# A two-layer hybrid encoder: the second layer's output projection with tokens on partitions, its input turned in blocks, and one attention set moved

## The reference

```python
m = jax.nn.sigmoid(mg).reshape(B, S, N_BRANCH, D_MODEL)
y = m[:, :, 0] * za + m[:, :, 1] * zb + m[:, :, 2] * zc
x = x + y @ w_out            # per layer
...
return rmsnorm(x, final_g)   # behind the second layer
```

## Time and profile before

| | |
|---|---|
| median of 3 runs | 967.1 us (966.6 to 967.12) |
| profiled execution: its time | 966.41 us |
| its span, first to last instruction | 964.3 us |
| busy in it: TensorE matmuls, VectorE, ScalarE | 956.2, 572.5, 401.7 us |
| clock granted to TensorE, mean | 1.000 of full speed |

### The profile page before, as it was taken

The page is one execution under the profiler, slowest core; times in us unless marked ns, Lnnn a source line. Parts: engine busy times, 40 slices in busy tenths (PEclk is TensorE's granted clock), DMA queues, the critical chain, the costliest instruction groups (busy, mean ns, idle before and its releaser), DMA issues.

```text
span 964.3 us, 13421 instructions
## 1 busy us (share of the span) xinstructions
PE 956.2 (99%) x5438; PEld 789.0 (82%) x5438; DVE 572.5 (59%) x933; ACT 401.7 (42%) x747; POOL 0.9 (0%) x5
## 2 busy tenths in 40 slices
PE   9999999999999999999999999999999999999997
PEld 7988888888888877788888888888888887878887
DVE  7856465447656577375566654744565665754844
ACT  7443343225633356432435323431463424653324
POOL 0000000000000000000000000000000000000000
PEclk9999999999999999999999999999999999999999
DMA  7423323222234211122322432223213332112212
GB/s 282 139 73 128 110 68 122 95 92 84 66 106 125 87 67 45 67 88 89 103 92 88 128 121 93 86 89 107 71 64 109 109 121 66 48 64 69 99 51 88
DMA packets 30237, 91.60 MB, mean 95 GB/s; under 512 B 4384, under 2 KB 7200, under 8 KB 30048
## 3 DMA queue, kind: packets, MB, share of 16 engines
q1 hardware_dynamic: 29184, 89.74, 27.8%
q10 hardware_dynamic: 992, 1.00, 0.4%
HBM read 84.89 MB, written 2.23 MB: 90 GB/s over the span
## 4 chain that ended last, share of the span: by engine, by line
PE 95%; DVE 2%; ACT 1%; DMA 1%; SPq 1%; issue 0%; DVEq 0%
PE ring L612 73%; PE nat L612 8%; PE nat L850 3%; PE aux L891 2%; PE nat L857 1%; PE nat L829 1%; PE nat L864 1%; DMA raw<-pieces 1%; ACT work L1123 1%; PE aux L710 1%; DVE merged L1181 1%; PE ring L633 0%; PE ring L634 0%; PE ring L635 0%; PE nat L792 0%
## 5 line engine op out<-in xcount | busy, mean ns | idle before, releaser
L612 PE MATMUL ring<-act_hi,w_hi 128*128 128x512 f32 x832 | 328.9, 395 | 0.0
L908 ACT ACTIVATE w_hi<-raw 128x1024 fp32r<-128x1024 f32 x152 | 161.8, 1064 | 392.3 <-PE ring L612 357.6
L612 PE MATMUL ring<-act_lo,w_hi 128*128 128x512 f32 x832 | 324.2, 390 | 0.0
L612 PE MATMUL ring<-act_hi,w_lo 128*128 128x512 f32 x832 | 324.1, 390 | 0.0
L1203 DVE TENSOR_TENSOR w_lo<-raw,w_hi 128x1024 fp32r<-128x1024 f32 x152 | 185.2, 1219 | 50.9 <-ACT w_hi L908 50.7
L612 PEld LDWEIGHTS ring<-act_hi,w_hi 128*128 128x128 f32 x832 | 156.2, 188 | 36.1 <-issue 4.9
L612 PEld LDWEIGHTS ring<-act_hi,w_lo 128*128 128x128 f32 x832 | 156.2, 188 | 33.0
L612 PEld LDWEIGHTS ring<-act_lo,w_hi 128*128 128x128 f32 x832 | 156.3, 188 | 31.0
L1525 DVE SCALAR_TENSOR_TENSOR gates<-ring,rstd 128x512 f32<-128x512 f32 x72 | 49.7, 690 | 130.1 <-PE ring L612 130.1
L612 PE MATMUL ring<-y_hi,w_hi 128*128 128x512 f32 x192 | 74.7, 389 | 0.0
L612 PE MATMUL ring<-y_lo,w_hi 128*128 128x512 f32 x192 | 74.7, 389 | 0.0
(11 more groups left out here) (227 smaller groups left out, 990.2 us busy)
## 6 DMA issues: line engine op xcount, KB each, us to landing
raw<-pieces SPq DMA_DIRECT2D x152, 512.0 KB, 3.5
xt<-x_t SPq DMA_DIRECT2D x8, 256.0 KB, 4.8
bank_a<-work SPq DMA_DIRECT2D x32, 64.0 KB, 2.0
out_t<-gates SPq DMA_DIRECT2D x7, 256.0 KB, 2.3
rope<-tables SPq DMA_DIRECT2D x1, 1024.0 KB, 6.1
bank_a<-work SPq DMA_DIRECT2D x32, 32.0 KB, 2.0
raw<-pieces SPq DMA_DIRECT2D x2, 256.0 KB, 5.0
bank_g<-k_rope_dram SPq DMA_DIRECT2D x8, 64.0 KB, 3.2
```

Source lines behind the costliest of these rows:

```text
L612: mm = pe.matmul(dst, stationary, moving, start=start and i == 0, stop=stop and i == 2)
L908: nc.scalar.activation(w_hi[:, n % HL, :], raw[:, n % RAW, :], ACT.Copy).then_inc(hi_split.sem, 1)
```

## The change

The order: set 0 of branch C is issued behind nine quarters instead of ten, and two quarters follow its `turn_c`. The last `y_lo` comes four quarters earlier. Both hold for both layers.

In layer 1 a new entry `turn_x` lets VectorE transpose the residual stream in blocks of 32 x 32 (eight instructions of 128 x 512), into the free `bank_a`. Sixteen transfers of 128 KB on SP, in four batches ahead of four weight loads, put the blocks in place, so that `x_rows` holds the residual with tokens on the partitions, the features in the order `ROWS_ORDER`. The weights of this projection are packed in that order, and one transfer of 512 KB brings the gain, repeated on all partitions.

All eight pieces of the output projection of layer 1 then run in `last_rows`, with the activations stationary and the weights moving. The first four pieces give the first 512 features of all four groups of 128 tokens, in the four `nat` banks; the last four give the other 512 features, in the three ring banks and `aux`, and the last two pieces of these go group by group. The norm runs along the free axis: ScalarE squares with an accumulated sum, takes the root and scales the first half of the features, VectorE adds, multiplies by the gain, takes the reciprocal and scales the second half. Each group leaves in two transfers as soon as it is scaled, the last one's first half from ScalarE's queue. Pool has nothing to do. The host restores the order of the features.

```diff
-    quarters(10)
+    quarters(9)
...
-        quarters(1)
+        quarters(1 if y > 0 else 2)
     todo.append(("value_c", len(C_SETS) - 1))
     quarters(1)
     todo.append(("y_hi", 2 * TT - 1))
-    quarters(len(fill) - 1)
+    quarters(2)
     todo.append(("y_lo", 2 * TT - 1))
-    quarters(1)
+    todo.append(("turn_x", 0))
+    quarters(3)
+    todo.append(("turn_x", 1))
+    quarters(len(fill))
...
+        x_blocks = bank_a[:, 0:4096].rearrange("p (m t j c) -> p t m j c", m=4, t=TT, j=KT)
+        x_rows = bank_g[:, :].rearrange("p (t d) -> p t d", t=TT)
+        out_first = gates[:, 0:TT, :]
+        rows_raw, out_second = gates[:, TT:2 * TT, :], gates[:, 2 * TT:3 * TT, :]
+        gain = merged[:, 0:2, :]
+        squares = work[:, 0:TT, :]
+        row_ss, row_bias, row_rstd = sums[:, :, 0:2], recip[:, 0:TT], recip[:, TT:2 * TT]
...
+                if layer == DEPTH - 1 and PW <= p < PW + 4:
+
+                    m = p - PW
+                    sp.wait_ge(x_turned.sem, KT)
+                    for b in range(4):
+                        sp.dma_start(x_rows[32 * m:32 * m + 32, :, 256 * b:256 * b + 256],
+                                     bank_a[32 * b:32 * b + 32, 1024 * m:1024 * m + 1024].rearrange("p (t d) -> p t d", t=TT)
+                                     ).then_inc(rows_placed.sem, 16)
+                elif layer == DEPTH - 1 and p == PW + 4:
+                    sp.wait_ge(merge_lo.sem, merge_lo.at(layer, KT))
+                    sp.dma_start(gain, final_g).then_inc(gain_loaded.sem, 16)
...
-            for n, hs in enumerate(halves):
-                for lo, hi in ((0, 2), (2, 4), (4, 6), (6, KT if n == 0 else DVE_TILES)):
-                    sp.wait_ge(scaled.sem, KT * n + hi)
-                    sp.dma_start(out_t[:, lo:hi, hs], gates[:, lo:hi, hs]).then_inc(out_sent[0].sem, 16)
-            sp.wait_ge(out_sent[0].sem, 16 * 8)
+            for t in range(TT):
+                sp.wait_ge(scaled_dve.sem, t + 1)
+                sp.dma_start(out[t, :, HALF:D], out_second[:, t, :]).then_inc(out_sent[0].sem, 16)
+                if t < TT - 1:
+                    sp.wait_ge(scaled_act.sem, t + 1)
+                    sp.dma_start(out[t, :, 0:HALF], out_first[:, t, :]).then_inc(out_sent[0].sem, 16)
+            sp.wait_ge(out_sent[0].sem, 16 * (2 * TT - 1))
             sp.wait_ge(out_sent[1].sem, 16)
-
-
-        @block.gpsimd
...
-            def last_pieces():
...
+            def last_rows():
+
+                layer, banks = DEPTH - 1, [*(r[:, :] for r in ring), aux[:, :]]
+
+                def row_tile(p, k, t, bank):
+
+                    slot, ts = (layer * PIECES + p) % HL, slice(t * P, (t + 1) * P)
+                    cols = slice(k % 2 * HALF, k % 2 * HALF + HALF)
+                    pe.matmul(bank, act_hi[:, k, ts], w_hi[:, slot, cols], start=k == 0, stop=False)
+                    pe.matmul(bank, act_lo[:, k, ts], w_hi[:, slot, cols], start=False, stop=False)
+                    return pe.matmul(bank, act_hi[:, k, ts], w_lo[:, slot, cols], start=False, stop=k == KT - 1)
+
+                for n in range(4):
+                    pe.wait_ge(lo_split.sem, lo_split.at(layer, PW + n + 1))
+                    for k in (2 * n, 2 * n + 1):
+                        pe.wait_ge(merge_lo.sem, merge_lo.at(layer, k + 1))
+                        for t in range(TT):
+                            mm = row_tile(PW + n, k, t, nat[t])
                     mm.then_inc(proj_done.sem, 1)
-                last_sum()
-                pe.wait_ge(diag_set.sem, 2)
-                spread_half(1, nat[1])
-                spread_half(1, nat[2])
-
...
+                pe.wait_ge(proj_free.sem, proj_free.at(layer, by_dve(first_output(PW))))
+                pe.wait_ge(o_read.sem, o_read.at(layer, 2 * TT))
+                for n in range(2):
+                    pe.wait_ge(lo_split.sem, lo_split.at(layer, PW + 4 + n + 1))
+                    for k in (2 * n, 2 * n + 1):
+                        for t in range(TT):
+                            mm = row_tile(PW + 4 + n, k, t, banks[t])
+                    mm.then_inc(proj_done.sem, 1)
+                for t in range(TT):
+                    for n in range(2, 4):
+                        if t == 0:
+                            pe.wait_ge(lo_split.sem, lo_split.at(layer, PW + 4 + n + 1))
+                        for k in (2 * n, 2 * n + 1):
+                            mm = row_tile(PW + 4 + n, k, t, banks[t])
+                    mm.then_inc(rows_done.sem, 1)
...
+                        if layer == DEPTH - 1 and p == PW + 3:
+                            for t in range(TT):
+                                act.wait_ge(rows_added.sem, t + 1)
+                                nc.scalar.activation(squares[:, t, :], out_first[:, t, :], ACT.Square,
+                                                     accum_out=row_ss[:, t, 0:1]).then_inc(rows_sq.sem, 1)
...
-            for j in range(KT - 2):
...
-            act.wait_ge(spread.sem, 3)
-            nc.scalar.activation(rstd[:, HALF:S], nat[2][:, HALF:S], ACT.Copy).then_inc(spread_copied.sem, 1)
-            act.wait_ge(scaled_pool.sem, 1)
-            act.dma_start(out_t[:, DVE_TILES:KT, HALF:S], gates[:, DVE_TILES:KT, HALF:S]).then_inc(out_sent[1].sem, 16)
+            act.wait_ge(rows_sq.sem, TT)
+            for t in range(TT):
+                act.wait_ge(rows_added.sem, TT + t + 1)
+                nc.scalar.activation(squares[:, t, :], rows_raw[:, t, :], ACT.Square,
+                                     accum_out=row_ss[:, t, 1:2]).then_inc(rows_sq.sem, 1)
+                act.wait_ge(rows_sq.sem, TT + t + 1)
+                act.wait_ge(rows_bias.sem, 1)
+                nc.scalar.activation(rstd_nat[:, t:t + 1], row_ss[:, t, 1:2], ACT.Sqrt, scale=1.0 / D,
+                                     bias=row_bias[:, t:t + 1]).then_inc(rows_std.sem, 1)
+                act.wait_ge(rows_rstd.sem, t + 1)
+                nc.scalar.activation(out_first[:, t, :], out_first[:, t, :], ACT.Copy,
+                                     scale=row_rstd[:, t:t + 1]).then_inc(scaled_act.sem, 1)
+            act.wait_ge(scaled_act.sem, TT)
+            act.dma_start(out[TT - 1, :, 0:HALF], out_first[:, TT - 1, :]).then_inc(out_sent[1].sem, 16)
...
+            def add_first_rows():
+
+                dve.wait_ge(rows_placed.sem, 16 * 16)
+                for t in range(TT):
+                    nc.vector.tensor_tensor(out_first[:, t, :], nat[t], x_rows[:, t, 0:HALF], ALU.add).then_inc(rows_added.sem, 1)
+
+            def gain_first_rows():
+
+                dve.wait_ge(gain_loaded.sem, 16)
+                for t in range(TT):
+                    dve.wait_ge(rows_sq.sem, t + 1)
+                    nc.vector.tensor_tensor(out_first[:, t, :], out_first[:, t, :], gain[:, 0, :],
+                                            ALU.mult).then_inc(rows_gained.sem, 1)
+                nc.vector.tensor_scalar(row_bias, row_ss[:, :, 0], 1.0 / D, EPS, ALU.mult, ALU.add).then_inc(rows_bias.sem, 1)
 
             def last_norm():
 
...
-                scale(1, range(DVE_TILES))
+                banks = [*(r[:, :] for r in ring), aux[:, :]]
+                dve.wait_ge(rows_gained.sem, TT)
+                for t in range(TT):
+                    dve.wait_ge(rows_done.sem, t + 1)
+                    nc.vector.tensor_tensor(rows_raw[:, t, :], banks[t], x_rows[:, t, HALF:D], ALU.add).then_inc(rows_added.sem, 1)
+                    dve.wait_ge(rows_added.sem, TT + t + 1)
+                    nc.vector.tensor_tensor(out_second[:, t, :], rows_raw[:, t, :], gain[:, 1, :],
+                                            ALU.mult).then_inc(rows_gained.sem, 1)
+                    dve.wait_ge(rows_std.sem, t + 1)
+                    nc.vector.reciprocal(row_rstd[:, t:t + 1], rstd_nat[:, t:t + 1]).then_inc(rows_rstd.sem, 1)
+                    dve.wait_ge(rows_rstd.sem, t + 1)
+                    nc.vector.tensor_scalar(out_second[:, t, :], out_second[:, t, :], row_rstd[:, t:t + 1], None,
+                                            ALU.mult).then_inc(scaled_dve.sem, 1)
...
+                    elif name == "turn_x" and layer == DEPTH - 1:
+                        for j in range(4 * i, 4 * i + 4):
+                            nc.vector.transpose(x_blocks[:, :, :, j, :],
+                                                xt[:, j, :].rearrange("p (t m c) -> p t m c", t=TT, m=4)).then_inc(x_turned.sem, 1)
...
-                        elif layer == DEPTH - 1 and p >= PIECES - 2:
-                            if p == PIECES - 1:
+                        elif layer == DEPTH - 1 and p >= PW:
+                            if p == PW + 3:
+                                evacuated(layer, p)
+                                add_first_rows()
+                            elif p == PW + 4:
+                                gain_first_rows()
+                            elif p == PIECES - 1:
...
```

(53 more changed lines are left out.)

77 lines of the change are left out of this document (6 added, 71 removed).

## The result

The changed kernel takes 959.53 us (959.34 to 959.83, 4 runs) beside 967.11 us of the kernel before (966.6 to 967.6, 4 runs): a ratio of 0.9922, interval 0.9905 to 0.9939. That is faster, as forecast, by 7.6 us where 5.9 were forecast. The profiled execution took 959.69 us with a span of 957.9.

A forecast was written before the change was run, and what follows sets the result against it. TensorE's queue bounds the kernel until the last matmul, then a 9.14 us chain across engines. Terms -1.2 - 1.84 - 2.85 = -5.9 give a 958.4 span, 960.5 profiled and a 961.2 us median; range 959.9 to 962.2 (0.66).

The forecast's parts named there:

- The moved set: Branch C's set 0 issued a quarter earlier removes a 0.6 us TensorE stall in each layer: -1.2 us.
- The rival in which the stall moves along: Branch C's copies still end 0.6 us after the scores could start, so the stall remains: 962.4 us, chance 0.10.
- The matmuls: Second layer's output projection: 192 matmuls of 512 columns at 0.2267 us each, no half pieces: -1.84 us.
- 12.72 us from 942.28 on: Old projection's last two pieces, run as half pieces with what stood between them, taking 12.72 us, to become 10.88.
- The chain of the last group: After the last matmul: add, square with sum, root, reciprocal and scaling of the last 128 tokens, with handoffs: 2.81 us.
- The rival with groups that run behind: In the projection's end, VectorE's rounds per token group lag behind the matmuls: 964.7 us, chance 0.08.
- What is hidden: Eight block transposes, sixteen placing transfers and the gain load fit beside TensorE's work before and during the projection: cost 0.
- the bank that was named: A ring bank, needed two outputs after the last gate, where late transposes would make TensorE wait; 4.7 us of lateness free.
- The formula: Transposes of t us each cost 8t - 6.3 - 4.7: idle stretches, then lateness the ring bank allows; nothing below t = 1.4.
- the last step, from the profiled execution to the median: Adding 0.7 us to the forecast profiled execution of 960.5, giving a median of 961.2.
- the last landing: At the kernel's end, two 256 KB transfers, one per queue, land in 3.0 us; bounds 2.3 to 3.5.
- a landing of 2.3 and nothing else: What the prediction gave as lying below 959.9: the kernel's last transfers landing in 2.3 us instead of 3.0.

The follow-up runs named there:

- e2: The kernel before with only set 0 of branch C moved one quarter earlier, in both layers: 965.09 us, ratio 0.9985.
- e3: The changed kernel with set 0 of branch C back at its old place: 961.15 us, ratio 0.9945 to the kernel before.
- e8: The changed kernel with the projection's last two pieces run piece by piece over the four groups, not group by group: 963.01 us.
- e4: The changed kernel with each of the eight block transposes issued three times, the extra ones into spare space: 963.9 us.
- e1: The kernel before, run again unchanged against itself: 966.62 us, ratio 0.9999.
- e6: The changed kernel with the last group's two halves leaving in one 512 KB transfer from SP: 960.35 us.
- e5: The changed kernel, run again unchanged: 960.03 us, ratio 0.9929 to the kernel before.

## Why the prediction was right in direction and off in size

**The moved set: right, the size a little too small.** 1.2 was forecast and called all that is there to gain; 1.36 and, in e2, 1.49 us were gained in the traces, and the one stop that was measured from start to start costs 0.69 to 0.71 where the wait in the list is 0.61. e2 and e3 show that the edit alone does it. The rival in which the stall moves along is out.

**The matmuls: right,** -1.84 forecast and measured, at the pitch taken from another stage of the kernel before. The check beside it, "12.72 us from 942.28 on", does not come out of the rows (they give 12.60 to the start of the last matmul, 12.88 to its end), and nothing else rests on it.

**The chain of the last group: right,** 2.81 forecast, 2.76 measured. The rival with groups that run behind is out: VectorE waits for the matmuls, and e8 shows the round by itself.

**What is hidden: right.** The transposes took 0.6 each and left VectorE idle time. The sixteen transfers landed in 4.2 us in place of the 2.3 to 3.5 used, and that cost nothing, with 10 us in hand. e4 uses up the idle time that hides the transposes, and TensorE waits for the bank that was named. The formula's 8 x 1.8 - 11 = 3.4 for e4 (0.6 three times) stands beside 3.1 between the spans and 3.9 between the medians.

**What failed** are two terms of the sum. Either of them, with its measured size, would have brought the forecast down by enough for a range of this width to hold the 959.53.

The larger one is the last step, from the profiled execution to the median: "The median of the runs is 967.1, 0.7 above that execution, so 961.2". This 0.7 belongs to three runs and one execution and not to the kernel. Larger samples of the kernel before have medians 0.2 to 0.5 above that execution; in e1 the profiled execution lies 0.26 above the median of its own runs, and the two profiled executions of the changed kernel lie 0.16 above and 0.0 from the medians of theirs. The step also kept 2.1 us around the span, of which the changed kernel has 1.8, for a reason that stays open. Of the 1.7 us between 961.2 and 959.53, this step has 0.7 + 0.16 + 0.32 = 1.2. The prediction names nothing for it in the range, although runs of one kernel lie 0.8 apart. It gives "a landing of 2.3 and nothing else" as what lies below 959.9, but by its own terms that landing takes 0.7 off and gives 960.5.

The other is the last landing: "I take 3.0, nearer to the latter, since both are in flight together". It took 2.5, and the part behind the scaling 2.99 in place of 3.48. The seven others of this size take 2.1 to 2.4 in the profile after. They leave in such pairs too, the first of a pair in 2.1 and the second in 2.3 to 2.4, so a second transfer takes 0.2 to 0.4 longer than a first, and the lower end of the bounds was the nearer one. A merged transfer of their joint size (e6) takes 3.2, not the 3.5 of the weight pieces that served as the upper end.

With these, the stalls' 0.16, the chain's 0.05 and a start that was 0.19 later, the span is 957.9 in place of 958.4. The miss itself is small: e5, the same kernel again, has 960.03, inside the range, so on which side of 959.9 a sample falls is within the scatter between samples. The two terms were off all the same, as the traces show, and both made the forecast too long.

## What to carry to other kernels

Where one engine is the bound nearly to the end, what lies behind its last instruction is a chain with few links: cost it link by link, and let the work end in portions that the next engine can finish in the time that one portion takes (here 2.40 us of work in 2.72). New work on the other engines costs nothing as long as their idle stretches hold it; compute how late it may be, and at which buffer the lateness would show. And carry a measured span to a median only with an offset from many runs, or with its scatter in the range.

## What the runs showed that I had not expected

- A transfer of 128 KB between 32 partitions within SBUF lands in 4.2 us (3.8 to 4.9), twice the 2.1 of an output transfer of 256 KB from 128 partitions. The Trainium skill, "SBUF — State Buffer", section "Door 1: The DMA port swizzle", says that a transfer's bandwidth depends on how many of the sixteen ports its partitions reach; these rows agree in direction, but no run varied the partitions alone, and the sixteen also stay within SBUF and go out four at a time behind a weight load.
- A transfer of 512 KB out of SBUF lands in 3.2 us, and a pair of 256 KB issued 0.24 to 0.37 us apart within 2.5 of the later issue and 2.8 of the first, from one queue or from two.
- A stop of TensorE costs more than the list of waits prints: 0.69 to 0.71 us from start to start for a wait of 0.61.
